# A two-stream transformer and state-space step on one core: the x chunks of groups 1 to 7 multiplied with high and low tokens side by side

## The chip, the cores and the metric

The kernel runs on one core of one Trainium2 chip. The metric is the device time of one execution in microseconds (us). The engines named here are TensorE (PE; its weight loads are PEld), VectorE (DVE), ScalarE (ACT), GpSimd (POOL) and SyncE (SP), which issues most of the loads of weights.

## The reference

Two streams of 128 tokens each (context and latent) go through two layers of width 2048. What matters here is the state-space branch of a layer:

```python
q, k, v, z_a, xbc, z_s, dt_f, dt_b, g_a, g_s = split_cols(h @ w_in, IN_SPLITS)
xbc = jax.nn.silu(centred_conv(xbc, conv_w, conv_b))      # 5 taps over the tokens, per channel
xs, b_ssm, c_ssm = split_cols(xbc, (SSD_WIDTH, BC_WIDTH, BC_WIDTH))
...
y = y_f + jnp.flip(y_b, 1) + d_skip[:, None].astype(x4.dtype) * x4
y = y.reshape(bsz, length, SSD_WIDTH) * jax.nn.silu(z_s)
yg = rmsnorm(y.reshape(bsz, length, N_SSD_GROUPS, SSD_WIDTH // N_SSD_GROUPS), ...)
```

`xs` has 4096 channels in 8 groups of 512. For each group the kernel computes its 512 columns of `h @ w_in` (a chunk called x), the convolution over the tokens, and then the two scans, which are matrix products with decay matrices.

## The kernel before, in words

**Chunks and halves.** Every product with a weight matrix is cut into chunks of 512 output columns, and a chunk into 8 halves (pieces of 256 x 512 weights, 128 x 1024 numbers in a tile). SyncE loads a half into one of 5 slots of `raw`. ScalarE rounds it into `w_h` (fp32r; `hi_half`, L473), VectorE forms the rest `w_l = raw - w_h` (`lo_half`, L478), and TensorE multiplies (`mm_half`): weights high times tokens high, weights high times tokens low, weights low times tokens high. `w_h` and `w_l` are rings of 4: ScalarE may split half k when TensorE has finished half k - 4 (semaphore `w_used`). Each engine's program is written out by hand: after half i of a chunk it does the steps listed for i. I number the 16 halves of a group 0 to 15.

**A group.** In the state-space stage a group g has two chunks: x (halves 0 to 7, channels on the partitions, accumulated in `pair(0)`, the first two banks of `PM`) and z_s (halves 8 to 15, tokens on the partitions, in the last two banks of `PM`). Between those halves the engines also do the scan of group g - 1. The steps that matter:

- TensorE: `y_start` and `xt_T` after half 0, `y_T` after 3, `y_diag` of two heads after 5, 7, 9 and 11 (into banks 0 and 1 of `A`; L816), `final_states` after 14 (into banks 2 and 3 of `A`).
- ScalarE: `z_silu` and `stores` after half 2, `clamp` (L1340) and `exp` (L1348) of four pairs of heads after 2 to 10, where the exponentials of the third and fourth pair wait for `y_diag` after halves 5 and 7, `y_hi` after 7 (L1355), the centre tap of the convolution after 11 (`conv`, L1394), its SiLU after 15 (L1401), then `squares` (L1369), which waits for VectorE's `add_y`. The split of half 0 of the next group stands behind `squares`.
- VectorE: `M` of the four pairs after 5, 7, 9 and 11 (three TENSOR_TENSOR each, L1601), `y_lo` after 8 (L1882), the four other taps after 12 and 13 (`conv_1`, `conv_2`, 16 instructions, L1645), `add_y` after 15 (three TENSOR_TENSOR).

**Another form that the kernel already has.** For the four z_a chunks of the attention stage `mm_wide` (L531 and L538) is used. A wide half holds 4 pieces of 128 rows by 256 columns: it multiplies each weight tile with high and low tokens side by side in one instruction of 512 columns (the two sums lie in the two halves of a bank), and only w_l times high tokens in one of 256. A chunk then has 4 halves for its first 256 channels and 4 for its last.

Of the kernel before, what the change touches and what calls it, by code (L numbers as in the profile page):

```python
# [17 lines left out]
ALU = mybir.AluOpType  # L18
# [5 lines left out]
TOK = 128  # L24
# [7 lines left out]
NG = 8  # L32
# [19 lines left out]
PH_SSD = PH_BC + 4  # L52
# [8 lines left out]
U_SSD = U_BC + 2  # L61
# [126 lines left out]
Z_RUN, Z_LOAD = z_tiles()  # L188


WIDE_BLOCKS = [B_ZA + g for g in range(4)]


def raw_order():
# [91 lines left out]
def build(nc, a, o):  # L286
    with ExitStack() as ctx:
# [505 lines left out]
        def _(pe):  # L793
# [33 lines left out]
            def layer(L, more):  # L827
# [175 lines left out]
                def ssd_steps(q):  # L1003
# [6 lines left out]
                    st[7] = st[7] + [lambda: banks_back(q)]  # L1010
                    return st

                def ssd_body(g, steps):
                    halves(base + PH_SSD + g * 2, "ch", 0, ub + U_SSD + g, hT_h, hT_l, steps)
# [155 lines left out]
        def _(act):  # L1170
# [40 lines left out]
            def layer(L, more):  # L1211
# [175 lines left out]
                def conv(g):  # L1387
                    chunk_done(act, base + PH_SSD + g * 2)
                    act.wait_ge(s_("chw_ready"), L + 1)
                    act.wait_ge(s_("conv_silu"), L * 12 + 4 + g)  # L1390
                    if g:
                        act.wait_ge(s_("xt_T"), L * NG + g)
                    for t in range(4):
                        mm = act.activation(xc[:, t * 256:(t + 1) * 256].rearrange("p (s n) -> p s n", s=2),  # L1394
                                            psum_sub(pair(0), t), F.Identity,
                                            bias=taps(5, 4 * g + t), scale=taps(2, 4 * g + t))
                    mm.then_inc(s_("conv_center"), 1)

                def silu(g):
# [186 lines left out]
        def _(dve):  # L1586
# [96 lines left out]
            def layer(L, more):  # L1683
# [70 lines left out]
                def conv_bc(k, half):  # L1754

                    freed, done, uses = ((bank_free[1], ub + U_BC + 2, 1), (bank_free[0], ub + U_BC + 3, 2),
                                         (s_("c_banks_read"), L + 1, 1), (bank_free[1], ub + U_BC + 3, 1))[k]
                    if half == 0:
                        dve.wait_ge(s_("conv_center"), L * 12 + k + 1)
# [127 lines left out]
                def ssd_steps(q):  # L1887
# [5 lines left out]
                        st[5 + 2 * p] = [lambda p=p: M(q, p)]  # L1893
                    return st

                def conv_1(g):
                    dve.wait_ge(s_("conv_center"), L * 12 + 4 + g + 1)
                    conv_taps(pair(0), 4 * g, bank_free[0], (0, 1))

                def conv_2(g):  # L1900
                    conv_taps(pair(0), 4 * g, bank_free[0], (3, 4))
                    dve.wait_ge(bank_free[0], ub + U_SSD + g + 2)
                    dve.sem_inc(s_("conv_done"), 1)

                def ssd_body(g, steps):
                    st = {k: list(v) for k, v in steps.items()}
                    st[12] = [lambda: conv_1(g)] + st.get(12, [])
                    st[13] = [lambda: conv_2(g)] + st.get(13, [])
# [377 lines left out]
```

## Time and profile before

| | |
|---|---|
| median of 3 runs | 2758.02 us (2757.69 to 2758.1) |
| the profiled execution | 2757.51 us, its span 2755.6 us |
| granted clock of TensorE, mean over the span | 0.996 |
| busy: PE, PEld, DVE, ACT, POOL | 98%, 83%, 72%, 54%, 6% |

The span is the time from the first to the last instruction; the profiled execution's own time is 1.9 us longer. Busy time is the sum of the instructions' spans; matmuls overlap in it. A timeline row gives the start and length of a run of like instructions, and in brackets how long the engine had been idle and what ended that.

### The profile page before, as it was taken

Reading aid. Unit: us, or ns where it says so; the run is one execution under the profiler, and the core shown is the slowest. Engines: PE = TensorE matmul, PEld = TensorE weight load, DVE = VectorE, ACT = ScalarE, POOL = GpSimd, SP = SyncE. Lnnn points to the kernel's source line nnn. Section 1 sums busy time; section 2 is a strip of 40 time slices with the busy share of each in tenths; the row PEclk is TensorE's granted clock in tenths of the full one; section 3 lists DMA queues with packets and bytes.
Section 4 is the critical chain, followed back from the end, with each engine's and each line's share of the span. In section 5 each row is a group of like instructions: output and inputs, shape, how many; then the busy total and the mean of one; then the engine's idle time right before and its main releaser. Section 6 shows DMA issues by size and latency. Waiting matters only on the chain.

```text
span 2755.6 us, 38506 instructions
## 1 busy us (share of the span) xinstructions
PE 2704.9 (98%) x15312; PEld 2297.9 (83%) x15312; DVE 1975.6 (72%) x2308; ACT 1490.4 (54%) x2161; POOL 172.5 (6%) x242
## 2 busy tenths in 40 slices
PE   6999999999999999999999999999999999999998
PEld 4898898888887888888879898889888888888886
DVE  2488788887997667688865788888866644655555
ACT  3366877785333455534434677787644344555443
POOL 0000101111000000000110011110110000000000
PEclk9999999999999999999999999999999999999999
DMA  9956666666987655587885666576566664545665
GB/s 393 345 178 219 218 223 211 201 226 233 316 307 274 229 192 191 187 289 264 306 282 174 202 221 222 191 234 219 190 229 237 244 199 161 176 160 184 201 218 168
DMA packets 175668, 627.84 MB, mean 228 GB/s; under 512 B 21029, under 2 KB 23333, under 8 KB 175105
## 3 DMA queue, kind: packets, MB, share of 16 engines
q1 hardware_dynamic: 154944, 557.19, 58.3%
q0 software_dynamic: 10672, 33.30, 4.2%
q10 hardware_dynamic: 9872, 34.89, 4.0%
q8 instruction: 121, 1.98, 0.3%
q14 instruction: 59, 0.48, 0.1%
HBM read 611.37 MB, written 13.93 MB: 227 GB/s over the span
## 4 chain that ended last, share of the span: by engine, by line
PE 88%; DVE 6%; DMA 3%; ACT 2%; issue 1%; SPq 0%; DVEq 0%; POOLq 0%; POOL 0%; ACTq 0%
PE PM L500 19%; PE PM L512 19%; PE PM L501 19%; PE A L816 6%; PE PM L516 5%; PE PM L505 5%; PE PM L506 5%; PE A L531 2%; PE PM L531 2%; DMA Zt<-in_w_mod 2%; DVE w_l L478 1%; DVE arena L598 1%; DVE X L1645 1%; DMA raw<-in_w_in 1%; PE PM L538 1%
## 5 line engine op out<-in xcount | busy, mean ns | idle before, releaser
L478 DVE TENSOR_TENSOR w_l<-raw,w_h 128x1024 fp32r<-128x1024 f32 (+1 forms) x880 | 1059.2, 1222 | 653.2 <-ACT w_h L473 645.7
L473 ACT ACTIVATE w_h<-raw 128x1024 fp32r<-128x1024 f32 (+1 forms) x880 | 905.5, 1046 | 759.0 <-PE PM L512 565.1
L500 PE MATMUL PM<-w_h,hT 128*128 128x512 f32 x1408 | 563.5, 400 | 2.1 <-issue 1.8
L501 PE MATMUL PM<-w_h,hT 128*128 128x512 f32 x1408 | 549.2, 390 | 0.0
L500 PE MATMUL PM<-w_h,Z 128*128 128x512 f32 x1016 | 399.2, 393 | 0.8 <-issue 0.8
L501 PE MATMUL PM<-w_h,Z 128*128 128x512 f32 x1016 | 395.6, 389 | 0.0
L512 PE MATMUL PM<-w_l,hT 128*128 128x512 f32 x1408 | 377.3, 390 | 0.0
L505 PE MATMUL PM<-hT,w_h 128*128 128x256 f32 x1408 | 350.6, 287 | 3.3 <-DVE X L1645 1.7
L506 PE MATMUL PM<-hT,w_h 128*128 128x256 f32 x1408 | 344.8, 283 | 0.0
L500 PEld LDWEIGHTS PM<-w_h,hT 128*128 128x128 f32 x1408 | 264.6, 188 | 59.7 <-issue 7.8
L512 PEld LDWEIGHTS PM<-w_l,hT 128*128 128x128 f32 x1408 | 264.2, 188 | 57.0 <-DVE w_l L478 0.4
L501 PEld LDWEIGHTS PM<-w_h,hT 128*128 128x128 f32 x1408 | 264.6, 188 | 55.8 <-issue 3.3
L505 PEld LDWEIGHTS PM<-hT,w_h 128*128 128x128 f32 x1408 | 269.2, 191 | 9.8 <-issue 5.5
L512 PE MATMUL PM<-w_l,Z 128*128 128x512 f32 x1016 | 272.5, 390 | 2.4 <-DVE w_l L478 2.4
L506 PEld LDWEIGHTS PM<-hT,w_h 128*128 128x128 f32 x1408 | 269.6, 192 | 0.5
L500 PEld LDWEIGHTS PM<-w_h,Z 128*128 128x128 f32 x1016 | 190.7, 188 | 44.2 <-issue 5.1
L512 PEld LDWEIGHTS PM<-w_l,Z 128*128 128x128 f32 x1016 | 190.1, 188 | 44.3 <-DVE w_l L478 4.5
L501 PEld LDWEIGHTS PM<-w_h,Z 128*128 128x128 f32 x1016 | 190.8, 188 | 40.1 <-issue 1.0
L516 PE MATMUL PM<-hT,w_l 128*128 128x256 f32 x1408 | 197.8, 283 | 0.9 <-DVE w_l L478 0.9
L516 PEld LDWEIGHTS PM<-hT,w_l 128*128 128x128 f32 x1408 | 181.6, 192 | 1.3 <-DVE w_l L478 1.3
L1340 ACT ACTIVATE Zt<-Zt,SA 128x128 f32<-128x128 f32 x512 | 162.5, 391 | 1.0 <-DMA Zt<-acs_scratch 0.9
L1601 DVE TENSOR_TENSOR arena<-arena 128x512 f32<-128x512 f32 (+2 forms) x158 | 142.4, 901 | 5.4
(215 smaller groups left out, 2612.1 us busy)
## 6 DMA issues: line engine op xcount, KB each, us to landing
raw<-in_w_in SPq DMA_DIRECT2D x608, 512.0 KB, 4.5
raw<-in_w_ps SPq DMA_DIRECT2D x128, 512.0 KB, 4.6
Zt<-in_w_mod SPq DMA_DIRECT2D x104, 512.0 KB, 13.2
arena<-in_w_mod SPq DMA_DIRECT2D x72, 512.0 KB, 6.5
Zt<-acs_scratch ACTq DMA_DIRECT2D x64, 512.0 KB, 4.8
raw<-in_w_pa SPq DMA_DIRECT2D x64, 512.0 KB, 4.2
raw<-in_w_out SPq DMA_DIRECT2D x64, 512.0 KB, 5.5
arena<-in_states POOLq DMA_DIRECT2D x16, 512.0 KB, 7.5
```

Source lines behind the costliest of these rows:

```text
L473: act.activation(w_h[:, k % RING, :, 0:n], half_raw(k, n), ACT.Copy).then_inc(hi_ready, 1)
L478: dve.tensor_tensor(w_l[:, k % RING, :, 0:n], half_raw(k, n), w_h[:, k % RING, :, 0:n].bitcast(F32), ALU.subtract).then_inc(lo_ready, 1)
L500: pe.matmul(tok_out(s), hi[:, kt, tk], wh, start=kt == 0, stop=False, skip_group_check=True)
L501: pe.matmul(tok_out(s), lo[:, kt, tk], wh, start=False, stop=False, skip_group_check=True)
L505: pe.matmul(ch_out(t), wh[:, cs], hi[:, kt], start=kt == 0 and t % 2 == 0, stop=False, skip_group_check=True)
L506: pe.matmul(ch_out(t), wh[:, cs], lo[:, kt], start=False, stop=False, skip_group_check=True)
L512: mm = pe.matmul(tok_out(s), hi[:, kt, s * TOK:(s + 1) * TOK], wl, start=False, stop=kt == last_kt, skip_group_check=True)
L516: mm = pe.matmul(ch_out(t), wl[:, t * P:(t + 1) * P], hi[:, kt], start=False, stop=kt == last_kt, skip_group_check=True)
L531: pe.matmul(banks[:, t, :].rearrange("p (x n) -> p x n", x=2), w[0][:, at:at + P], hT[:, :, kt], start=kt == 0, stop=False, skip_group_che ...
L816: return pe.matmul(out, lhsT, rhs, start=start, stop=stop, skip_group_check=True)
L1340: ins = act.activation(rows_of[:, ds], rows_of[:, ds], F.Relu, scale=-1.0, bias=SA[:, ds, q * HG + h:q * HG + h + 1])
L1601: return dve.tensor_tensor(out, a_, b_, op)
```

## The change

The x chunks of groups 1 to 7, in both layers, are done by `mm_wide`. Halves 0 to 3 of the chunk go into `pair(0)` and halves 4 to 7 into banks 2 and 3 of `A`. Weights of these blocks are laid out for it ahead of the launch. The high and low sums then have to be added: ScalarE copies the low sum of two tiles to `x_low` in `Zt` (`copy_low`, after half 8 and after half 11), VectorE adds it to the high sum in PSUM, in place (`sum_x`, after half 10 and after half 11), ScalarE makes the centre tap in two parts (`center_x`, after halves 11 and 12), and VectorE the other taps, from PSUM, in two parts (`conv_x`, after halves 12 and 13). Group 0 stays as it was.

```diff
-WIDE_BLOCKS = [B_ZA + g for g in range(4)]
+WIDE_BLOCKS = [B_XBC + g for g in range(1, NG)] + [B_ZA + g for g in range(4)]
...
+        def x_summed_at(t):
+            return (PM if t < 2 else A)[:, t, 0:256].rearrange("p (s n) -> p s n", s=2)
...
                 def final_states(q):
                     if q:
                         pe.wait_ge(s_("st_stored"), L * NG + q)
+                    if q < NG - 1:
+                        pe.wait_ge(s_("conv_done"), L * 12 + 4 + q + 2)
...
+                def x_wide(g, steps):
+                    c = base + PH_SSD + g * 2
+                    bank_wait(pe, 0, ub + U_SSD + g)
+                    for i in range(8):
+                        if i == 4 and g > 1:
+                            pe.wait_ge(s_("st_stored"), L * NG + g - 1)
+                        mm_wide(pe, c, i, pair(0) if i < 4 else A[:, 2:4, :])
...
+                def copy_low(g, part):
+                    chunk_done(act, base + PH_SSD + g * 2, 4 + 4 * part)
+                    if part == 0:
+                        act.wait_ge(s_("conv_done"), L * 12 + 4 + g)
+                    banks = A[:, 2:4, :] if part else pair(0)
+                    act.activation(x_low[:, part * 512:(part + 1) * 512]..., banks[:, :, 256:512], F.Copy)
+                def center_x(g, part):
+                    if part == 0:
+                        act.wait_ge(s_("conv_silu"), L * 12 + 4 + g)
+                        act.wait_ge(s_("xt_T"), L * NG + g)
+                    act.wait_ge(s_("x_summed"), 2 * (L * (NG - 1) + g - 1) + part + 1)
+                    for t in (2 * part, 2 * part + 1):
+                        mm = act.activation(x_tile(xc, t), x_summed_at(t), F.Identity, bias=..., scale=...)
...
-                    st[11] = [lambda: conv(g)] + st.get(11, [])
+                    if g:
+                        st[8] = st.get(8, []) + [lambda: copy_low(g, 0)]
+                        st[11] = [lambda: copy_low(g, 1), lambda: center_x(g, 0)] + st.get(11, [])
+                        st[12] = [lambda: center_x(g, 1)] + st.get(12, [])
...
+                def sum_x(g, part):
+                    dve.wait_ge(s_("x_low_copied"), 2 * (L * (NG - 1) + g - 1) + part + 1)
+                    high = A[:, 2:4, 0:256] if part else PM[:, 0:2, 0:256]
+                    tt(high, high, low, ALU.add).then_inc(s_("x_summed"), 1)
+                def conv_x(g, part):
+                    tiles = (2 * part, 2 * part + 1)
+                    ...
+                            ins = dve.scalar_tensor_tensor(out=o_, in0=x_summed_at(t)[:, :, lo_ + d:hi_ + d], ...)
+                    ins.then_inc(s_("conv_done") if part else bank_free[0], 1)
...
+                    if g:
+                        st[10] = st.get(10, []) + [lambda: sum_x(g, 0)]
+                        st[11] = [lambda: sum_x(g, 1)] + st.get(11, [])
+                        st[12] = [lambda: conv_x(g, 0)] + st.get(12, [])
+                        st[13] = [lambda: conv_x(g, 1)] + st.get(13, [])
```

On ScalarE, from the exponential of the third pair (L1348 before, L1373 now) to the split of half 12, these rows stood in group 2 before (L473 is the split into `w_h`, L1340 a clamp, L1394 the centre tap):

```order
L1348 ACTIVATE arena<-Zt 128x1024 [waits act_chain,y_part]
L1340 ACTIVATE Zt<-Zt,SA 128x128 [waits decays_loaded1]
L1340 ACTIVATE Zt<-Zt,SA 128x128 x3
L473 ACTIVATE w_h<-raw 128x1024 [waits w_used,raw_loaded2]
L1277 DMA Zt<-acs_scratch 128x1024 [waits exp_done]
L1340 ACTIVATE Zt<-Zt,SA 128x128 x4
L473 ACTIVATE w_h<-raw 128x1024 [waits w_used,raw_loaded3]
L1348 ACTIVATE arena<-Zt 128x1024 [waits act_chain,y_part]
L473 ACTIVATE w_h<-raw 128x1024 [waits w_used,raw_loaded4]
L1394 ACTIVATE X<-PM,chw 128x256 [waits conv_silu,xt_T,chw_ready,w_used]
L1394 ACTIVATE X<-PM,chw 128x256 x3
```

And now (L475 is the split, L1365 a clamp, L1428 the copy of a low sum, L1437 the centre tap):

```order
L1373 ACTIVATE arena<-Zt 128x1024 [waits act_chain,y_part]
L1365 ACTIVATE Zt<-Zt,SA 128x128 [waits decays_loaded1]
L1365 ACTIVATE Zt<-Zt,SA 128x128 x3
L1428 ACTIVATE Zt<-PM 128x512 [waits conv_done,w_used]
L475 ACTIVATE w_h<-raw 128x1024 [waits w_used,raw_loaded2]
L1302 DMA Zt<-acs_scratch 128x1024 [waits exp_done]
L1365 ACTIVATE Zt<-Zt,SA 128x128 x4
L475 ACTIVATE w_h<-raw 128x1024 [waits w_used,raw_loaded3]
L1373 ACTIVATE arena<-Zt 128x1024 [waits act_chain,y_part]
L475 ACTIVATE w_h<-raw 128x1024 [waits w_used,raw_loaded4]
L1428 ACTIVATE Zt<-A 128x512 [waits w_used]
L1437 ACTIVATE X<-PM,chw 128x256 [waits x_summed,xt_T,conv_silu]
```

The first copy of a low sum stands ahead of the split of half 9, the second behind that of half 11, and the centre tap now waits for VectorE.

On VectorE, from the split of half 10 to the split of half 14, these rows stood in group 2 before (L478 the split into `w_l`, L1645 the taps):

```order
L478 TENSOR_TENSOR w_l<-raw,w_h 128x1024 [waits hi_ready] x2
L1601 TENSOR_TENSOR arena<-arena,SA 128x1024 [waits exp_done]
L1601 TENSOR_TENSOR arena<-arena 128x1024 [waits dve_chain]
L1601 TENSOR_TENSOR arena<-arena 128x2x256 [waits dve_chain]
L478 TENSOR_TENSOR w_l<-raw,w_h 128x1024 [waits hi_ready]
L1645 SCALAR_TENSOR_TENSOR X<-PM,chw,X 128x2x126 [waits conv_center]
L1645 SCALAR_TENSOR_TENSOR X<-PM,chw,X 128x2x126 x3
L1645 SCALAR_TENSOR_TENSOR X<-PM,chw,X 128x2x127 [waits dve_chain] x4
L478 TENSOR_TENSOR w_l<-raw,w_h 128x1024 [waits hi_ready]
L1645 SCALAR_TENSOR_TENSOR X<-PM,chw,X 128x2x127 [waits dve_chain] x4
L1645 SCALAR_TENSOR_TENSOR X<-PM,chw,X 128x2x126 [waits dve_chain] x4
L478 TENSOR_TENSOR w_l<-raw,w_h 128x1024 [waits bank_free0,hi_ready]
```

And now (L480 the split, L1647 the sums and products, L1961 the taps):

```order
L480 TENSOR_TENSOR w_l<-raw,w_h 128x1024 [waits hi_ready]
L1647 TENSOR_TENSOR PM<-PM,Zt 128x2x256 [waits x_low_copied]
L480 TENSOR_TENSOR w_l<-raw,w_h 128x1024 [waits hi_ready]
L1647 TENSOR_TENSOR A<-A,Zt 128x2x256 [waits x_low_copied]
L1647 TENSOR_TENSOR arena<-arena,SA 128x1024 [waits exp_done]
L1647 TENSOR_TENSOR arena<-arena 128x1024 [waits dve_chain]
L1647 TENSOR_TENSOR arena<-arena 128x2x256 [waits dve_chain]
L480 TENSOR_TENSOR w_l<-raw,w_h 128x1024 [waits hi_ready]
L1961 SCALAR_TENSOR_TENSOR X<-PM,chw,X 128x2x126 [waits x_summed,conv_center]
```

Two sums stand ahead of the fourth `M`, and the split of half 14 no longer waits for `bank_free0`, which the second part of the taps used to release and wait for.

## Rows read from the trace of the kernel before

**Rows 1.** The page, busy time, share of the span and instructions of each engine.
```profile
PE 2704.9 (98%) x15312; PEld 2297.9 (83%) x15312; DVE 1975.6 (72%) x2308; ACT 1490.4 (54%) x2161; POOL 172.5 (6%) x242
```

**Rows 2.** What TensorE waited for: us in total, times, longest.
```profile
PE PM L505 <- ACT w_h L473: 1.0, 2, 0.5
```

**Rows 3.** Busy time by engine in one group: PE, PEld, DVE, ACT, POOL, PEclk, DMA.
```profile
332.76:386.47 53.71, 53.71 (x346) 47.80 (x344) 45.87 (x59) 40.48 (x72) 6.84 (x8) 1.00 0.64 216
```

**Rows 4.** Timeline of TensorE: start us, length us, line, count.
```profile
332.76 0.28 PE L505 MATMUL PM<-hT,w_h 128*128 128x256 f32 x1
...
349.63 1.12 PE L516 MATMUL PM<-hT,w_l 128*128 128x256 f32 x8
352.51 1.12 PE L516 MATMUL PM<-hT,w_l 128*128 128x256 f32 x8
353.48 1.00 PE L816 MATMUL A<-X,arena 128*128 128x64 f32 x8
...
360.12 1.00 PE L816 MATMUL A<-X,arena 128*128 128x64 f32 x8
...
386.47 0.28 PE L505 MATMUL PM<-hT,w_h 128*128 128x256 f32 x1
...
547.59 0.28 PE L505 MATMUL PM<-hT,w_h 128*128 128x256 f32 x1
...
601.72 0.47 PE L500 MATMUL PM<-w_h,hT 128*128 128x512 f32 x1 [0.26 <-issue]
```

**Rows 5.** Timeline of ScalarE in the same group, and one row at 599 us.
```profile
328.76 0.63 ACT L1369 ACTIVATE arena<-X 128x512 f32<-128x512 f32 x1 [4.50 <-DVE X L1601]
...
352.67 1.07 ACT L473 ACTIVATE w_h<-raw 128x1024 fp32r<-128x1024 f32 x1
354.51 1.06 ACT L1348 ACTIVATE arena<-Zt 128x1024 f32<-128x1024 f32 x1 [0.78 <-PE A L816]
...
356.65 1.05 ACT L473 ACTIVATE w_h<-raw 128x1024 fp32r<-128x1024 f32 x1
...
361.16 1.06 ACT L1348 ACTIVATE arena<-Zt 128x1024 f32<-128x1024 f32 x1 [1.34 <-PE A L816]
...
382.46 0.63 ACT L1369 ACTIVATE arena<-X 128x512 f32<-128x512 f32 x1 [4.50 <-DVE X L1601]
...
384.11 2.96 ACT L473 ACTIVATE w_h<-raw 128x1024 fp32r<-128x1024 f32 x3
...
599.17 2.96 ACT L473 ACTIVATE w_h<-raw 128x1024 fp32r<-128x1024 f32 x3 [0.17 <-issue]
```

**Rows 6.** Timeline of VectorE in the same group.
```profile
355.69 1.65 DVE L1882 SCALAR_TENSOR_TENSOR Z<-PM,chw,Z 128x256 fp32r<-128x256 f32 x4
357.73 1.23 DVE L478 TENSOR_TENSOR w_l<-raw,w_h 128x1024 fp32r<-128x1024 f32 x1 [0.39 <-ACT w_h L473]
...
361.99 2.44 DVE L478 TENSOR_TENSOR w_l<-raw,w_h 128x1024 fp32r<-128x1024 f32 x2
...
373.61 3.19 DVE L1645 SCALAR_TENSOR_TENSOR X<-PM,chw,X 128x254 f32<-128x254 f32 x8
376.94 2.36 DVE L478 TENSOR_TENSOR w_l<-raw,w_h 128x1024 fp32r<-128x1024 f32 x2
...
381.20 1.23 DVE L1601 TENSOR_TENSOR X<-X 128x1024 f32<-128x1024 f32 x1
```

**Rows 7.** Waits of ScalarE for VectorE, whole span: us in total, times, longest.
```profile
ACT arena L1369 <- DVE X L1601: 69.9, 16, 4.5
```

**Rows 8.** Timeline of TensorE in a z_a chunk.
```profile
949.99 2.00 PE L531 MATMUL PM<-hT,w_h 128*128 128x512 f32 x8
...
952.78 2.00 PE L531 MATMUL PM<-hT,w_h 128*128 128x512 f32 x8
```

**Rows 9.** A pair of half-size VectorE products (timeline), and ScalarE's copies in z_a (source view).
```profile
342.98 1.28 DVE L1601 TENSOR_TENSOR arena<-A,SA 128x512 f32<-128x512 f32 x2
...
L1514 ACT ACTIVATE arena<-PM x8: 598/598/599, 958.6 to 2458.4; 128x512 f32<-128x512 f32 x8
```

More of the change, by code:

```diff
@@ L323, in part @@
             return arena[:, at:at + n]
+        CENTERS = 5 + 2 * (NG - 1)
         BCX = part(4352, 0).rearrange("p (t n) -> p t n", n=256)
@@ L334, in build @@
         decay_rows = [Zt[:, 7, :], Zt[:, 15, :]]
+        x_low = Zt[:, 6, :]
         def CB(q):
@@ L693, in psum_sub, with x_tile @@
             return banks[:, t // 2, (t % 2) * 256:(t % 2 + 1) * 256].rearrange("p (s n) -> p s n", s=2)
+        def x_tile(held, t):
+            return held[:, t * 256:(t + 1) * 256].rearrange("p (s n) -> p s n", s=2)
+        def x_summed_at(t):
+            return (PM if t < 2 else A)[:, t, 0:256].rearrange("p (s n) -> p s n", s=2)
         def x_banks(q):
@@ L1011, in ssd_steps @@
                     return st
+                def x_wide(g, steps):
[5 more added lines that the diff above has]
+                        mm_wide(pe, c, i, pair(0) if i < 4 else A[:, 2:4, :])
+                        tiles_behind(K(c, i))
+                        for step in steps.get(i, ()):
+                            step()
                 def ssd_body(g, steps):
-                    halves(base + PH_SSD + g * 2, "ch", 0, ub + U_SSD + g, hT_h, hT_l, steps)
+                    if g:
+                        x_wide(g, steps)
+                    else:
+                        halves(base + PH_SSD, "ch", 0, ub + U_SSD, hT_h, hT_l, steps)
                     halves(base + PH_SSD + g * 2 + 1, "tok", 1, ub + U_SSD + g, hT_h, hT_l, steps, first=8)
@@ L1390, in conv @@
                     act.wait_ge(s_("conv_silu"), L * 12 + 4 + g)
-                    if g:
-                        act.wait_ge(s_("xt_T"), L * NG + g)
                     for t in range(4):
@@ L1396, in conv @@
                                             bias=taps(5, 4 * g + t), scale=taps(2, 4 * g + t))
+                    mm.then_inc(s_("conv_center"), 1)
+                def copy_low(g, part):
[3 more added lines that the diff above has]
+                    banks = A[:, 2:4, :] if part else pair(0)
+                    act.activation(x_low[:, part * 512:(part + 1) * 512].rearrange("p (t n) -> p t n", t=2), banks[:, :, 256:512], F.Copy)                        .then_inc(s_("x_low_copied"), 1)
+                def center_x(g, part):
[4 more added lines that the diff above has]
+                    for t in (2 * part, 2 * part + 1):
+                        mm = act.activation(x_tile(xc, t), x_summed_at(t), F.Identity, bias=taps(5, 4 * g + t), scale=taps(2, 4 * g + t))
                     mm.then_inc(s_("conv_center"), 1)
@@ L1758, in conv_bc @@
                     if half == 0:
-                        dve.wait_ge(s_("conv_center"), L * 12 + k + 1)
+                        dve.wait_ge(s_("conv_center"), L * CENTERS + k + 1)
                     conv_taps(bc_banks(k), 32 + 4 * k, freed, ((0, 1), (3, 4))[half], uses)
@@ L1894, in ssd_steps @@
                     return st
+                def sum_x(g, part):
+                    dve.wait_ge(s_("x_low_copied"), 2 * (L * (NG - 1) + g - 1) + part + 1)
+                    low = x_low[:, part * 512:(part + 1) * 512].rearrange("p (t n) -> p t n", t=2)
+                    high = A[:, 2:4, 0:256] if part else PM[:, 0:2, 0:256]
+                    tt(high, high, low, ALU.add).then_inc(s_("x_summed"), 1)
+                def conv_x(g, part):
+                    tiles = (2 * part, 2 * part + 1)
+                    dve.wait_ge(s_("conv_center"), L * CENTERS + 5 + 2 * (g - 1) + part + 1)
+                    dve.wait_ge(s_("x_summed"), 2 * (L * (NG - 1) + g - 1) + part + 1)
+                    for j in (0, 1, 3, 4):
+                        d = j - 2
+                        lo_, hi_ = max(0, -d), TOK - max(0, d)
+                        for t in tiles:
+                            if j > 0:
+                                ch.wait(tap_done[t])
+                            o_ = x_tile(xc, t)[:, :, lo_:hi_]
+                            ins = dve.scalar_tensor_tensor(out=o_, in0=x_summed_at(t)[:, :, lo_ + d:hi_ + d], scalar=taps(j, 4 * g + t),
+                                                           in1=o_, op0=ALU.mult, op1=ALU.add)
+                            if not (j == 4 and t % 2):
+                                tap_done[t] = ch.link(ins)
+                    ins.then_inc(s_("conv_done") if part else bank_free[0], 1)
                 def conv_1(g):
-                    dve.wait_ge(s_("conv_center"), L * 12 + 4 + g + 1)
+                    dve.wait_ge(s_("conv_center"), L * CENTERS + 5)
                     conv_taps(pair(0), 4 * g, bank_free[0], (0, 1))
@@ L1906, in ssd_body @@
                     st = {k: list(v) for k, v in steps.items()}
-                    st[12] = [lambda: conv_1(g)] + st.get(12, [])
-                    st[13] = [lambda: conv_2(g)] + st.get(13, [])
+                    if g:
+                        st[10] = st.get(10, []) + [lambda: sum_x(g, 0)]
+                        st[11] = [lambda: sum_x(g, 1)] + st.get(11, [])
+                        st[12] = [lambda: conv_x(g, 0)] + st.get(12, [])
+                        st[13] = [lambda: conv_x(g, 1)] + st.get(13, [])
+                    else:
+                        st[12] = [lambda: conv_1(g)] + st.get(12, [])
+                        st[13] = [lambda: conv_2(g)] + st.get(13, [])
                     halves(base + PH_SSD + g * 2, st)
```

2 lines of the change are left out of this document (added).

## The prediction

> **What bounds the kernel now.** I read the page first: TensorE is busy for 98% of the span, VectorE for 72%, ScalarE for 54% [rows 1]. The waits of TensorE are next: in the whole program it waited for ScalarE's split 1.0 us in 2 waits ahead of the matmuls of an x chunk [rows 2]. So TensorE sets the time, and one group of the state-space stage, from the first matmul of its half 0 at 332.76 to that of the next at 386.47, takes 53.71 us [rows 3, 4], with no gap.
>
> That it never waits doesn't say how near it is to waiting. For that I followed the two engines that feed it. After the scan of a group ScalarE sits idle for 4.50 us until VectorE has ended `add_y`, then does `squares`, and only behind that splits half 0 of the next group [rows 5]. All 16 `squares` wait like this, 69.9 us in total [rows 7], so the pattern repeats at every boundary. The first of the three splits starts at 384.11 and, at some 1.06 us each, has ended at 385.17; TensorE needs it at 386.47. The slack is 1.30 us.
>
> From one `squares` to the next there is thus a loop through ScalarE and VectorE, and I measure it. I call the start of `squares` S (328.76).
> - ScalarE works without a gap from S to the split of half 8, which ends at 353.74 [rows 5]. The next ACTIVATE could start 0.10 earlier than that (three splits of 1.05 take 2.96), at S + 24.88. It started at 354.51, for it waited 0.78 us for `y_diag`, which ended at 353.48 + 1.00 [rows 4].
> - From there to the split of half 9 are 2.14 us (356.65 - 354.51), and its end is 1.05 later.
> - VectorE is ready for half 9 when `y_lo` has ended (355.69 + 1.65, less its overlap of 0.08), at S + 28.50; it waited 0.39 us for that split and started at 357.73 [rows 6].
> - From 357.73 VectorE is busy to the end of `add_y` (381.20 + 1.23), and `squares` starts at 382.46: 24.73 us.
>
> If TensorE never held it, the loop would take 28.50 + 24.73 = 53.23 us, just 0.48 less than TensorE's 53.71. The kernel has two limits here that lie within 1% of each other.
>
> **The change, part by part.**
> 1. TensorE's saving. A half of the x chunk takes 352.51 - 349.63 = 2.88 us, 24 matmuls of 256 columns [rows 4]. A wide half, 8 of 512 and 8 of 256, takes 952.78 - 949.99 = 2.79 [rows 8]. That is 0.09 a half, 0.72 a group, 10.1 us over 14 chunks. TensorE's own time for a group falls to 52.99.
> 2. ScalarE's first copy of a low sum. Such a copy takes 598 ns [rows 9], 0.50 less the overlap. It stands ahead of the split of half 9. That split then ends at S + 24.88 + 2.14 + 0.50 + 1.05 = S + 28.57 and VectorE starts on it at S + 28.60, against S + 28.50: plus 0.10 on the loop (where `y_diag` was the last to come, as in group 1, plus the whole 0.50).
> 3. VectorE's two sums. No row shows a sum written to PSUM. The nearest are two 512-element products with one operand from PSUM in 1.28 us, 0.60 each with the overlap [rows 9]. I take 0.60 each, so plus 1.20: both stand in VectorE's unbroken stretch. Bounds: a single-input pass of this size costs about 0.4, and a sum at half rate would be like one of twice the elements, 1.23 with 0.08 overlap, 1.15. That makes 0.8 to 2.3 for the two. Nothing at all is excluded, since the stretch has no gap to hide them in.
> 4. What goes. The splits of halves 10 and 11 now take 2.44, of which 0.08 is a wait for ScalarE (2 x 1.22 less overlap is 2.36); behind the first sum that wait is gone: minus 0.08. Between the last tap (373.61 + 3.19 = 376.80) and the split of half 14 (376.94) lie 0.14, where the overlap would be 0.08; the wait for `bank_free0` there is gone: minus 0.22.
> 5. At no cost: the second copy (after half 11; VectorE needs it three microseconds later), the centre tap in two parts (four instructions before and after, its wait for the sums falls into ScalarE's idle time, and the taps need it only behind `M`), the 16 taps (two tiles at a time, so an instruction depends on the one two before it, 0.78 us earlier, and one takes under 0.5). TensorE's new wait for `st_stored` at half 4 is covered, because ScalarE stores ahead of the split of half 3, and that for `conv_done` because the split of half 14 stands behind the same taps. Loads keep their sizes and order. If the cover of the centre tap were gone, its two instructions, 0.9, would come onto the loop.
>
> **The sum.** The loop becomes 28.60 + 24.73 + 1.20 - 0.08 - 0.22 = 54.23 us, above TensorE's 52.99 and above 53.71. Is `y_diag` then still early enough? TensorE starts half 0 at S + 2.71 (385.17 - 382.46). `y_diag` ended 354.48 - 332.76 = 21.72 after that start, now 0.54 less (six shorter halves): S + 23.89, before ScalarE's S + 24.88. The fourth pair: 361.12 - 332.76 - 0.72 + 2.71 = S + 30.35, ScalarE comes at S + 24.88 + 5.31 + 0.50 = S + 30.69 (5.31 is 361.16 - 1.34 - 354.51). So the loop holds itself, and TensorE waits for the split of half 0, 54.23 - 52.99 = 1.24 us a group.
>
> By boundary, in each layer:
> - Out of group 1, whose ScalarE has no stores and waits for `y_diag`: the split comes 0.50 + 1.20 - 0.30 = 1.40 later, TensorE is 0.18 earlier (two halves after `y_diag`), the slack was 1.30: a wait of 0.28. Net -0.72 + 0.28 = -0.44.
> - Groups 2 to 6: 54.23 - 53.71 = +0.52 each, +2.60.
> - Group 7, into the next stage: it took 601.72 - 547.59 = 54.13, and ScalarE pays 0.2 more at the end of the phase (0.17 of idle time ahead of its splits) [rows 4, 5]: 54.23 + 0.2 - 54.13 = +0.3.
>
> That is +2.5 a layer, +5.0 in all. The later stages have no such loop and keep what they are given. The profiled execution's 2757.5 would become 2762.5; the runs' median lies 0.5 above it, so I forecast **2763.0 us**. 0.2% of this kernel, about what a measurement can tell from no change, is 5.5 us: the forecast lies just inside it, on the slow side.
>
> A rule would make TensorE's part smaller. The row gives 0.09 us a half. The Trainium skill, VectorE: DVE Perf Modes, in its section on the TRN2 errata, has a matmul take 6 cycles plus its columns; by it 8 x 216 + 8 x 109 ns against 24 x 109 would save 0.02 us a half, 2 us in all, and the sum would end at about 2764, since the saving counts in group 1 alone. The trace has its own durations, and I use those.
>
> **The rivals.**
> - *TensorE's saving comes through.* For it speaks that TensorE is busy for all 53.71 us of a group and VectorE for 45.87 (85%), which the sums raise to 47.1 [rows 3]: by busy shares there is room. It holds if the loop stays below 52.99. It is 53.23 - 0.30 = 52.93 without the new work, so the new work would have to cost under 0.1 where I count 1.30. Then the time is 2758.0 - 10.1 = 2747.9. Against it speak the loop's gapless rows. The Trainium skill, Perfetto Trace Analysis, section Identifying the Most-Contended Engine, says to find the limit by occupancy and work on that engine first; by that rule it is TensorE, and this rival is what it gives. Chance 12% for over 0.2% faster.
> - *Loop and saving cancel.* The added work comes to about 0.8 us a loop in place of 1.30: 53.73 a group, as before, and about 2757. It decides at this price of 0.8: below it the kernel gains, above it it loses. Chance 20%.
> - *The loop as worked out*, 2763, its own range 2759 to 2768. Chance 50%.
> - *Slower by more: sums in PSUM at half rate.* At 1.15 each the loop grows by 1.10 more, 54.23 + 1.10 = 55.33, in six boundaries of a layer, with the first too: 14 x 1.1 = 15 us, 2778. Also here belongs the split of half 14, at S + 50.0 against TensorE's need at S + 50.3, by my sum: if that is missed, TensorE waits in mid-group, which its 1.24 of waiting at half 0 pays for until it's used up. Chance 18% for above 2768.
>
> **How the numbers follow.** The likeliest case gives 2763.0. Between 2756 and 2770 lie the loop, most of the cancelling case and the lower third of the last one, some 8 in 10. Faster by over 0.2% (below 2752.5): 0.12. Slower by over 0.2% (above 2763.5): the upper part of the loop's case, 0.25, and the last, 0.18, makes 0.43. Within: 0.45.
>
> **What the changed profile would show.** Right: groups 2 to 6 some 54.2 us apart; TensorE idle for 1.2 us at each boundary until ScalarE's split, about 12 waits; the wide halves 2.79 apart; VectorE's sums 0.68 long; ScalarE's exponential of the third pair no longer waiting for `y_diag`. Wrong: groups at 53.0 with no idle TensorE (the saving came through), sums of over 1 us, a gap ahead of the sums or taps (a copy or centre tap is late), or waits in mid-group at halves 4 or 14. The forecast is wrong above all if the price of the sums or the overlaps of 0.1 are off: each 0.1 us in the loop is 1.4 us in the total.

## The result, and the profile after

The changed kernel takes **2762.16 us** (median of 14 runs, 2761.02 to 2765.98), the kernel before 2758.19 (14 runs, 2757.16 to 2759.03) beside it. The ratio is 1.0016, with a 95% interval of 1.0009 to 1.0024: slower by 4.0 us, or 0.16%. Forecast were 2763.0 and a range of 2756 to 2770. The profiled execution took 2761.81 us, its span 2760.0.

The page of after, busy time by engine, answers to [rows 1]; under it stands the line of section 4, the chain that ended last by engine:

```profile
PE 2702.2 (98%) x14416; PEld 2253.2 (82%) x14416; DVE 1990.6 (72%) x2336; ACT 1501.3 (54%) x2189; POOL 172.1 (6%) x242
...
PE 67%; DVE 21%; ACT 5%; issue 4%; DMA 3%; SPq 0%; DVEq 0%; ACTq 0%; POOLq 0%; POOL 0%
```

TensorE does 896 matmuls fewer and is busy for 2.7 us less, in a program that takes 4 us more. The shares look like those of before. The chain does not: VectorE now holds 21% of it, and in the chain of before it held 6%:

```profile
PE 88%; DVE 6%; DMA 3%; ACT 2%; issue 1%; SPq 0%; DVEq 0%; POOLq 0%; POOL 0%; ACTq 0%
```

This share is a hint and no price: experiment 1 has one nearly as large without a wait at half 0. What TensorE waited for at half 0 (us in total, times, longest) answers to [rows 2]:

```profile
PE PM L533 <- ACT w_h L475: 8.9, 12, 1.1
```

That is the predicted number of waits: six boundaries in each of the two layers. (The seventh, out of group 7, leads to a chunk of another form and stands at L502.) The windows view of group 2, half 0 to half 0 (length, then PE, PEld, DVE, ACT, POOL, granted clock, DMA share, GB/s), answers to [rows 3]:

```profile
332.52:386.65 54.13, 53.31 (x280) 44.40 (x281) 46.84 (x61) 41.28 (x74) 6.83 (x9) 1.00 0.66 214
```

A group takes 54.13 us where it took 53.71, at a granted clock of 1.00, the level of 2.4 GHz, and TensorE has gaps in it. Its timeline shows them at the first matmul of half 0 (L533). The columns are start, length, line and count, and in brackets the idle time and what ended it; this answers to [rows 4]. (The last row is cut off at the end of the view, so it counts 3 of its 8 matmuls.)

```profile
332.52 2.09 PE L533 MATMUL PM<-hT,w_h 128*128 128x512 f32 x8 [0.85 <-ACT w_h L475]
...
337.91 2.09 PE L533 MATMUL PM<-hT,w_h 128*128 128x512 f32 x8
...
340.79 2.00 PE L533 MATMUL PM<-hT,w_h 128*128 128x512 f32 x8
...
343.58 2.00 PE L533 MATMUL PM<-hT,w_h 128*128 128x512 f32 x8
...
352.84 1.00 PE L824 MATMUL A<-X,arena 128*128 128x64 f32 x8
...
386.65 0.94 PE L533 MATMUL PM<-hT,w_h 128*128 128x512 f32 x3 [0.82 <-ACT w_h L475]
```

The wide form does work faster: half 2 follows at 340.79 and half 3 at 343.58, 2.79 apart, against 2.88 before. But half 0 now waits for ScalarE's split, at every boundary. ScalarE's timeline of the same group answers to [rows 5]:

```profile
329.66 0.63 ACT L1394 ACTIVATE arena<-X 128x512 f32<-128x512 f32 x1 [4.32 <-DVE X L1647]
...
354.51 1.06 ACT L1373 ACTIVATE arena<-Zt 128x1024 f32<-128x1024 f32 x1
356.63 0.59 ACT L1428 ACTIVATE Zt<-PM 128x512 f32<-128x512 f32 x1
357.11 1.06 ACT L475 ACTIVATE w_h<-raw 128x1024 fp32r<-128x1024 f32 x1
...
364.41 0.56 ACT L1437 ACTIVATE X<-PM,chw 128x256 f32<-128x256 f32 x1 [1.56 <-DVE PM L1647]
...
383.79 0.63 ACT L1394 ACTIVATE arena<-X 128x512 f32<-128x512 f32 x1 [4.32 <-DVE X L1647]
...
385.45 2.96 ACT L475 ACTIVATE w_h<-raw 128x1024 fp32r<-128x1024 f32 x3
```

The first of the three splits takes some 1.06 us and ends at 386.51; TensorE starts at 386.65. The slack at half 0, 1.30 before, is 0.14 at all seven boundaries of a layer: so much remains when the split is what is waited for. The exponential of the third pair (354.51) no longer has a bracket: `y_diag`, ended at 352.84 + 1.00 = 353.84, is not awaited any more. From one `squares` to the next are 383.79 - 329.66 = 54.13 us, exactly TensorE's period. VectorE's timeline answers to [rows 6]:

```profile
356.59 1.66 DVE L1928 SCALAR_TENSOR_TENSOR Z<-PM,chw,Z 128x256 fp32r<-128x256 f32 x4
358.20 1.23 DVE L480 TENSOR_TENSOR w_l<-raw,w_h 128x1024 fp32r<-128x1024 f32 x1
...
363.60 0.69 DVE L1647 TENSOR_TENSOR PM<-PM,Zt 128x512 f32<-128x512 f32 x1
364.20 1.22 DVE L480 TENSOR_TENSOR w_l<-raw,w_h 128x1024 fp32r<-128x1024 f32 x1
365.34 0.69 DVE L1647 TENSOR_TENSOR A<-A,Zt 128x512 f32<-128x512 f32 x1
365.94 1.22 DVE L1647 TENSOR_TENSOR arena<-arena,SA 128x1024 f32<-128x1024 f32 x1
...
375.19 3.19 DVE L1961 SCALAR_TENSOR_TENSOR X<-A,chw,X 128x252 f32<-128x252 f32 x8
378.30 2.35 DVE L480 TENSOR_TENSOR w_l<-raw,w_h 128x1024 fp32r<-128x1024 f32 x2
...
382.54 1.22 DVE L1647 TENSOR_TENSOR X<-X 128x1024 f32<-128x1024 f32 x1
```

There is no bracket in the whole stretch from 356.59 to 382.54: VectorE doesn't wait once. Each sum takes 0.69, and the next instruction starts 0.60 after the start of the sum.

### The profile page after: what moved, and what is told of

It is laid out like the page before. It is cut to its first block, busy times and chain, and to the rows that moved or that the text cites. A ratio compares the mean times of both kernels' runs of the same rounds, so it can differ in the third digit from the quotient of the medians.

```text
span 2760.0 us, 36798 instructions
## 1 busy us (share of the span) xinstructions
PE 2702.2 (98%) x14416; PEld 2253.2 (82%) x14416; DVE 1990.6 (72%) x2336; ACT 1501.3 (54%) x2189; POOL 172.1 (6%) x242
## 4 chain that ended last, share of the span: by engine, by line
PE 67%; DVE 21%; ACT 5%; issue 4%; DMA 3%; SPq 0%; DVEq 0%; ACTq 0%; POOLq 0%; POOL 0%
PE PM L502 15%; PE PM L514 15%; PE PM L503 15%; DVE w_l L480 6%; DVE arena L1647 4%; PE PM L533 4%; PE A L824 4%; PE A L533 4%; DVE arena L600 3%; PE PM L540 2%; PE A L540 2%; ACT w_h L475 2%; DVE X L1961 2%; DMA Zt<-in_w_mod 2%; DVE X L600 1%
## 5 line engine op out<-in xcount | busy, mean ns | idle before, releaser
L480 DVE TENSOR_TENSOR w_l<-raw,w_h 128x1024 fp32r<-128x1024 f32 (+1 forms) x880 | 1060.1, 1223 | 640.3 <-ACT w_h L475 635.2
L475 ACT ACTIVATE w_h<-raw 128x1024 fp32r<-128x1024 f32 (+1 forms) x880 | 905.2, 1046 | 730.8 <-PE PM L514 540.3
L502 PE MATMUL PM<-w_h,hT 128*128 128x512 f32 x1408 | 563.9, 400 | 3.6 <-ACT w_h L475 2.1
L502 PE MATMUL PM<-w_h,Z 128*128 128x512 f32 x1016 | 399.5, 393 | 0.8 <-issue 0.8
L502 PEld LDWEIGHTS PM<-w_h,hT 128*128 128x128 f32 x1408 | 264.8, 188 | 61.1 <-issue 9.3
L502 PEld LDWEIGHTS PM<-w_h,Z 128*128 128x128 f32 x1016 | 190.8, 188 | 44.1 <-issue 5.1
L533 PE MATMUL PM<-hT,w_h 128*128 128x512 f32 x704 | 180.7, 399 | 8.9 <-ACT w_h L475 8.9
L533 PE MATMUL A<-hT,w_h 128*128 128x512 f32 x704 | 179.2, 397 | 0.0
L1365 ACT ACTIVATE Zt<-Zt,SA 128x128 f32<-128x128 f32 x512 | 162.5, 392 | 0.2 <-DMA Zt<-acs_scratch 0.2
L533 PEld LDWEIGHTS PM<-hT,w_h 128*128 128x128 f32 x704 | 127.1, 189 | 39.2 <-issue 16.5
L1647 DVE TENSOR_TENSOR arena<-arena 128x512 f32<-128x512 f32 (+2 forms) x158 | 142.4, 901 | 5.3
L533 PEld LDWEIGHTS A<-hT,w_h 128*128 128x128 f32 x704 | 126.4, 189 | 22.5
L507 PE MATMUL PM<-hT,w_h 128*128 128x256 f32 x512 | 128.1, 288 | 3.3 <-DVE X L1691 1.7
L508 PE MATMUL PM<-hT,w_h 128*128 128x256 f32 x512 | 125.4, 283 | 0.0
```

The costliest lines, as they stand in the source:

```text
L475: act.activation(w_h[:, k % RING, :, 0:n], half_raw(k, n), ACT.Copy).then_inc(hi_ready, 1)
L480: dve.tensor_tensor(w_l[:, k % RING, :, 0:n], half_raw(k, n), w_h[:, k % RING, :, 0:n].bitcast(F32), ALU.subtract).then_inc(lo_ready, 1)
L502: pe.matmul(tok_out(s), hi[:, kt, tk], wh, start=kt == 0, stop=False, skip_group_check=True)
L507: pe.matmul(ch_out(t), wh[:, cs], hi[:, kt], start=kt == 0 and t % 2 == 0, stop=False, skip_group_check=True)
L508: pe.matmul(ch_out(t), wh[:, cs], lo[:, kt], start=False, stop=False, skip_group_check=True)
L533: pe.matmul(banks[:, t, :].rearrange("p (x n) -> p x n", x=2), w[0][:, at:at + P], hT[:, :, kt], start=kt == 0, stop=False, skip_group_che ...
```

## The experiments

The theory on trial: the loop from `squares` through the scan's splits, VectorE's unbroken stretch and back to `squares` sets the time of a group, because the split of half 0 stands behind `squares` on ScalarE. The rivals: the wide form or the sums' traffic in PSUM hold TensorE by themselves; the place of `squares` costs something in any case; VectorE or ScalarE have simply too much to do. The kernel before took 2757.95 us beside the first four kernels (15 runs, 2756.77 to 2759.41) and 2757.98 beside the last four (15 runs, 2756.74 to 2758.7).

**1. The two sums left out.** This kernel leaves the low sum of x out of the result; copies, the centre tap, the taps and all semaphores stay.

```diff
-                    tt(high, high, low, ALU.add).then_inc(s_("x_summed"), 1)
+                    dve.sem_inc(s_("x_summed"), 1)
```

> The changed kernel without VectorE's 28 sums of the low to the high product of x: the copied low sum is left out of the computation, all waits and copies stay. Loop theory (the loop from one squares to the next through ScalarE and VectorE, 54.13 us measured in the changed kernel, sets the group): it shrinks by two sums of 0.60 to about 52.95, under TensorE's own time for a group, which is 53.1 to 53.15 by the idle 0.99 us of each boundary. Groups 2 to 6 come 53.1 to 53.2 apart, TensorE hardly waits at half 0, and the time is about 2750 us. Rival (the wide form itself costs the time, by its waits for PSUM banks and the later release of them): the sums are hidden, and the time stays within 2 us of 2762.

Measured: 2749.36 us (2748.11 to 2749.84), ratio to before 0.9968 (0.9955 to 0.9980). TensorE's timeline at two boundaries:

```profile
330.92 1.98 PE L533 MATMUL PM<-hT,w_h 128*128 128x512 f32 x8
...
383.96 1.98 PE L533 MATMUL PM<-hT,w_h 128*128 128x512 f32 x8
```

The groups are 53.04 apart here (53.03 on the mean of the layer), the bracket is gone, and the 8 matmuls take 1.98 instead of 2.09. The slack at half 0 is 0.98. So the wide form costs nothing hidden, and TensorE's own time for a group is 53.03: the saving is 0.68 a group. Two instructions of 0.69 us on an engine that is busy for 72% of the span hold back the whole of it. This alone doesn't separate the loop from "too much work on VectorE"; the next kernel does. The page's chain of this kernel, where TensorE waits at no half 0, still gives much to the two feeding engines, so their share of the chain isn't the time that they cost:

```profile
PE 63%; DVE 17%; ACT 12%; issue 5%; DMA 2%; SPq 0%; ACTq 0%; DVEq 0%; POOLq 0%; POOL 0%
```

**2. All the work kept, the loop cut.** `squares` moves behind the splits of halves 0 to 2 of the next group. It is what the split of half 0 stood behind; nothing is left out.

```diff
                     if q:
+                        st[2].insert(0, lambda: squares(q - 1))
                         st[2].append(lambda: stores(q - 1))
...
-                    if g:
-                        st[15].append(lambda: squares(g - 1))
```

> The changed kernel with ScalarE's squares of group g moved from behind half 15 to behind the split of half 2 of the next group. Nothing is left out. Loop theory: ScalarE makes three splits in the 4.3 us in which it waited for VectorE, so that 2.9 us leave the way from squares to the third exponential and the loop falls clearly under 53. TensorE is the limit again at 53.1 to 53.2 a group, its saving comes through, and the time is about 2750 us, faster than both kernels. Rival (the sums and copies lengthen VectorE's and ScalarE's work in a way that is paid wherever squares stand, or the wide form's own waits cost): 2760 to 2763.

Measured: 2748.53 us (2747.39 to 2749.81), ratio 0.9965 (0.9952 to 0.9977). TensorE's timeline, and ScalarE's at the end of the group:

```profile
331.62 1.98 PE L533 MATMUL PM<-hT,w_h 128*128 128x512 f32 x8
...
384.65 1.98 PE L533 MATMUL PM<-hT,w_h 128*128 128x512 f32 x8
```
```profile
378.07 2.01 ACT L475 ACTIVATE w_h<-raw 128x1024 fp32r<-128x1024 f32 x2 [0.25 <-remote]
380.43 1.06 ACT L475 ACTIVATE w_h<-raw 128x1024 fp32r<-128x1024 f32 x1 [0.34 <-PE PM L514]
382.14 0.63 ACT L1394 ACTIVATE arena<-X 128x512 f32<-128x512 f32 x1 [0.66 <-DVE X L1646]
```

The splits of halves 0 and 1 start at 378.07, the first of them ends at about 379.13, and half 0 is multiplied at 384.65: a slack of 5.5. ScalarE waits for VectorE only 0.66 where it waited 4.32, since it spends that time on splits. The windows view of a group says what "too much work" would have meant:

```profile
331.62:384.65 53.03, 53.03 (x281) 44.47 (x280) 46.87 (x61) 41.68 (x73) 7.88 (x9) 1.00 0.65 218
```

VectorE is busy for 46.87, with both sums, as in after (46.84), and the group takes 1.10 less. The amount of work didn't matter, its place in the loop did. This version beats both kernels: 9.4 us under the kernel before, where 14 chunks at 0.68 make 9.5.

**3. The same move on the kernel before**, with the same edit.

> The kernel before with squares moved in the same way. Nothing is left out. Loop theory: TensorE set its groups at 53.71 with 1.30 us of slack at half 0; more slack gives nothing, 2758.2 within 1 us. Rival (the place of squares costs something by itself, whatever the x chunk's form): 2 us or more faster, and then the gain of the second run would be no sign of the loop.

Measured: 2757.55 us (2756.98 to 2758.61), ratio 0.9999 (0.9990 to 1.0008). TensorE's timeline, and the split of half 0 on ScalarE's:

```profile
332.48 0.28 PE L505 MATMUL PM<-hT,w_h 128*128 128x256 f32 x1
...
386.19 0.28 PE L505 MATMUL PM<-hT,w_h 128*128 128x256 f32 x1
```
```profile
377.92 1.06 ACT L473 ACTIVATE w_h<-raw 128x1024 fp32r<-128x1024 f32 x1 [0.25 <-remote]
```

The groups stay 53.71 apart, with a slack of 7.2 at half 0. So the place of `squares` by itself is worth nothing; it pays only once TensorE needs less than the loop.

**4. The copies and sums on the kernel before.** The x chunk stays in its old form; ScalarE copies 512 columns of `A` after halves 8 and 11, and VectorE adds them in place after halves 10 and 11, where after has its copies and sums. They work on banks that nothing else uses at that time, and nothing of the output changes; in the first such group they take 384 columns.

```diff
+                        st[8] = st.get(8, []) + [lambda: copy_low(g, 0)]
+                        st[11] = [lambda: copy_low(g, 1), lambda: conv(g)] + st.get(11, [])
...
+                    if g:
+                        st[10] = st.get(10, []) + [lambda: sum_x(g, 0)]
+                        st[11] = [lambda: sum_x(g, 1)] + st.get(11, [])
```

> The kernel before with the new work alone: in groups 1 to 7 ScalarE copies two PSUM banks of 512 to the spare tile after halves 8 and 11 and VectorE adds them in PSUM after halves 10 and 11 (old final states, already stored, that nothing reads again), while the x chunk stays in its old form. Loop theory: the loop of 53.23 grows by 0.10 + 1.20 - 0.08 to 54.45 (54.35 if it is as much shorter than my sum as it was in the changed kernel), above TensorE's 53.71, so groups 2 to 6 come 54.3 to 54.5 apart and the time is about 2766. Rival (work on engines that are busy 85% and 75% of a group fits into their idle time): 2758.

Measured: 2766.54 us (2766.35 to 2768.74), ratio 1.0034 (1.0021 to 1.0046). TensorE's timeline at two boundaries:

```profile
334.75 0.36 PE L506 MATMUL PM<-hT,w_h 128*128 128x256 f32 x1 [0.43 <-ACT w_h L474]
...
389.11 0.36 PE L506 MATMUL PM<-hT,w_h 128*128 128x256 f32 x1 [0.43 <-ACT w_h L474]
```

They are 54.36 apart, TensorE waits for the same split, and the slack is the same 0.14. TensorE's own group is 0.68 longer here than in the changed kernel, but the time from group to group only by 0.23: the loop decides, not the matmuls. And the 0.23 has a place, in VectorE's timeline between the last tap and the split of half 14:

```profile
377.41 3.19 DVE L1658 SCALAR_TENSOR_TENSOR X<-PM,chw,X 128x254 f32<-128x254 f32 x8
380.74 2.36 DVE L479 TENSOR_TENSOR w_l<-raw,w_h 128x1024 fp32r<-128x1024 f32 x2
```

The taps end at 380.60 and the split starts 0.14 later, as before the change [rows 6]; in after it starts 0.08 ahead of their end. That is the wait for `bank_free0`, which this kernel keeps: 0.22, as the prediction had it.

**5. The sums doubled.** Each sum is made once more ahead of itself, into an unused slot of `Zt` in SBUF.

```diff
+                    tt(Zt[:, 14, part * 512:(part + 1) * 512]..., high, low, ALU.add)
                     tt(high, high, low, ALU.add).then_inc(s_("x_summed"), 1)
```

> The changed kernel with each of its 28 sums done twice, once more into a spare tile that nothing reads. Loop theory: a sum costs the loop its 0.60 to 0.61 us, so 1.21 more per group: groups 2 to 6 come 55.3 us apart in place of 54.13, TensorE waits 2.3 us at each boundary, and the time is 2762 + 14 x 1.21 = 2779. Rival (the extra time in the changed kernel is a fixed one per group, from the new waits between the engines, and the sums themselves are partly hidden): clearly less, 2762 to 2772.

Measured: 2779.56 us (2778.47 to 2780.07), ratio 1.0079 (1.0066 to 1.0092). VectorE's timeline, the two forms of the sum, and TensorE's timeline at two boundaries and at half 14:

```profile
366.09 0.68 DVE L1647 TENSOR_TENSOR Zt<-PM,Zt 128x512 f32<-128x512 f32 x1
366.69 0.69 DVE L1647 TENSOR_TENSOR PM<-PM,Zt 128x512 f32<-128x512 f32 x1
```
```profile
335.02 2.09 PE L533 MATMUL PM<-hT,w_h 128*128 128x512 f32 x8 [1.43 <-ACT w_h L475]
...
383.25 1.20 PE L514 MATMUL PM<-w_l,hT 128*128 128x512 f32 x4 [0.32 <-DVE w_l L480]
...
390.34 2.06 PE L533 MATMUL PM<-hT,w_h 128*128 128x512 f32 x8 [1.42 <-ACT w_h L475]
```

The groups are 55.32 apart (one, held up by a late transfer, took 56.37): 1.19 more than in after, for two more sums at 0.60. These sums are paid in full. The wait at half 0 grew by only about 0.6; the other part now stands in the middle of the group, where TensorE waits for VectorE's split of half 14 (0.32 in this row). The prediction had named that place as the next to give way. In after its split is there 0.76 ahead of TensorE (the sum had 0.3), here 0.06.

**6. The sums doubled and the loop cut**, the edits of 5 and 2 together.

> Doubled sums and squares behind the split of half 2, both. Loop theory: with squares out of the way the same 28 further sums, 17 us of VectorE's work, fit into VectorE's waits; the tightest place is the split of half 14, which had 1.40 us to spare with single sums and keeps 0.2. TensorE sets 53.03 a group, and the time is as with single sums, 2748 to 2750. Rival (VectorE's load as such has become the limit): 2755 or more.

Measured: 2748.65 us (2747.79 to 2750.17), ratio 0.9968 (0.9956 to 0.9981), as fast as experiment 2. TensorE's timeline:

```profile
331.81 1.98 PE L533 MATMUL PM<-hT,w_h 128*128 128x512 f32 x8
...
384.85 1.98 PE L533 MATMUL PM<-hT,w_h 128*128 128x512 f32 x8
```

The extra sums that cost 17 us in the loop cost nothing here. The slack is not unlimited: at half 14 VectorE's split is there just 0.21 ahead of TensorE.

**7. `squares` behind one split only**, to ask how far it has to move: `st[0].append(lambda: squares(q - 1))` in place of the line in `st[2]`.

> The changed kernel with squares moved behind the split of half 0 alone, not of half 2. Loop theory: only 0.95 us leave the way from squares to the third exponential, so the loop is 53.18 and still 0.15 over TensorE's 53.03, but TensorE no longer needs its split of half 0 from behind squares, and that of half 1 has 2.7 us more; the drift of 0.15 a group over six groups stays inside that. TensorE is the limit: 2748 to 2750. Rival (what counts is ScalarE's whole load in the 4.3 us gap, so one split of three gives a third of the gain): 2757 to 2759.

Measured: 2748.52 us (2747.64 to 2748.66), ratio 0.9966 (0.9953 to 0.9978). The groups are 53.03 apart. One split ahead of it is enough, but not for ever: the slack at half 0 shrinks from 5.49 to 4.88 over the groups of a layer, and that at half 14 from 1.40 to 0.69, some 0.1 a group. ScalarE's timeline shows why:

```profile
275.56 0.63 ACT L1394 ACTIVATE arena<-X 128x512 f32<-128x512 f32 x1 [2.98 <-DVE X L1646]
...
328.70 0.64 ACT L1394 ACTIVATE arena<-X 128x512 f32<-128x512 f32 x1 [2.98 <-DVE X L1646]
```

From one `squares` to the next are 53.14 us, 0.1 more than TensorE's 53.03; 53.18 was expected. The loop is still the longer one and eats the slack, but eight groups are too few for it to get through. With `squares` behind half 2 there is no such drift (5.50 at the first boundary and 5.50 at the sixth, half 14 at 1.40 in all groups but one, which has 1.14), so I would choose that place.

**8. The first copy behind the split of half 9**, for the 0.10 that it put on the loop.

```diff
-                        st[8] = st.get(8, []) + [lambda: copy_low(g, 0)]
+                        st[9] = [lambda: copy_low(g, 0)] + st.get(9, [])
```

> The changed kernel with ScalarE's first copy of the low sum behind the split of half 9 in place of ahead of it. Loop theory: in groups 2 to 6 the copy costs next to nothing where it is, for VectorE is ready for half 9 only at the time when the split ends, so the loop falls by 0.0 to 0.1 only (54.03 to 54.13); in group 1, where VectorE waits for it, the boundary to group 2 comes 0.3 to 0.5 earlier. In all 1 to 2 us, 2760 to 2761. Rival (the copy is paid in full, 0.50 a group): 2755.

Measured: 2760.35 us (2759.08 to 2762.08), ratio 1.0010 (1.0001 to 1.0019). ScalarE's timeline, and VectorE's:

```profile
356.35 1.06 ACT L475 ACTIVATE w_h<-raw 128x1024 fp32r<-128x1024 f32 x1
357.30 0.59 ACT L1428 ACTIVATE Zt<-PM 128x512 f32<-128x512 f32 x1
```
```profile
356.21 1.65 DVE L1928 SCALAR_TENSOR_TENSOR Z<-PM,chw,Z 128x256 fp32r<-128x256 f32 x4
357.78 1.21 DVE L480 TENSOR_TENSOR w_l<-raw,w_h 128x1024 fp32r<-128x1024 f32 x1
```

Now `y_lo` sets VectorE's start, not the split: the row behind it starts 0.08 ahead of its end. Most groups are 54.06 to 54.08 apart, some 0.06 less than in after. In each layer group 2 takes 53.95 or 53.97, some 0.17 less, and group 1 0.35 less (52.17 against 52.52 in layer 0). Ten groups (3 to 7) at 0.06, two at 0.17 and two at 0.35 make 1.6 us; the medians differ by 1.8. Two groups of the profiled execution took longer, 54.28 and 54.85; in both ScalarE waited for a late transfer (0.18 and 0.75). So the copy's place is a small term, as the sum had it, and the sums are nearly all of the loss.

## Why the prediction held, step by step

- **What bounds the kernel.** Two limits within 1% of each other: right. Experiment 3 shows that TensorE sets the time of before (nothing gained by cutting the loop), experiment 4 that the loop lies close behind it.
- **TensorE's saving**, forecast 0.72 a group, measured 0.68 (53.71 - 53.03, experiments 1 and 2): 9.5 us in place of 10.1. The two rows that I compared, 2.88 against 2.79, hold for a half that follows another. Behind other work the gain is less: half 1 stands behind `y_start` and `xt_T`. The trace of before has its first matmul and that of half 2 at

```profile
338.15 0.36 PE L505 MATMUL PM<-hT,w_h 128*128 128x256 f32 x1
...
341.10 0.28 PE L505 MATMUL PM<-hT,w_h 128*128 128x256 f32 x1
```

  that is 2.95, and now it takes 340.79 - 337.91 = 2.88: 0.07 in place of 0.09. Three halves of each x chunk (1, 4 and 6) stand so.
- **A rule on a matmul's length.** The Trainium skill, VectorE: DVE Perf Modes, section on the TRN2 errata, has a matmul take 6 cycles plus its columns; the estimate from it was 0.02 us saved a half. The runs don't agree: they show 0.68 / 8 = 0.085 a half, and the measurement decides.
- **The copy.** VectorE was to start on half 9 at S + 28.60 and started at 358.20 - 329.66 = S + 28.54. The exponential ahead of it, forecast at S + 24.88, came at S + 24.85. Experiment 8 puts the copy at 0.06 a loop (forecast 0.10) and 0.35 at the first boundary (forecast 0.50, the full copy).
- **The sums**, 0.60 each, were bounded between 0.8 and 2.3 for the two. Measured: 0.60 each, whether the result goes to PSUM or to SBUF (experiment 5), and 1.19 of loop for two of them.
- **What goes.** The rest of the loop was to take 24.73 + 1.20 - 0.08 - 0.22 = 25.63 and took 54.13 - 28.54 = 25.59.
- **The loop** therefore came to 54.13 where I had 54.23, against TensorE's 53.03 where I had 52.99. The wait is the difference of the two: 1.10 a boundary, forecast 1.24. The bracket shows 0.82 to 0.85 of it. Without a wait the first matmul starts 0.17 ahead of the end of the row before (384.65 against 383.74 + 1.08 in experiment 2), and behind a wait half 0 itself is 0.11 longer (from its start to that of half 1: 5.39 against 5.28).
- **At no cost.** The centre tap waits 1.56 for the sum, in ScalarE's idle time, and the taps behind it start without a bracket. `y_diag` came 0.67 ahead of ScalarE (forecast 0.99). TensorE's matmuls at half 4 (`A`, L533) and its `final_states` don't stand in the waits view at all.
- **By boundary**, layer 0: out of group 1, -0.33 (52.52 against 52.85; forecast -0.44). Groups 2 to 6, +0.42 each (forecast +0.52). Group 7, +0.22 (54.35 against 54.13; forecast +0.3). That is +2.0, and +2.2 in layer 1, where one group took 54.39: 4.2 of the 4.4 us by which the span grew, where I had 5.0. The ten middle boundaries at 0.10 less make 1.0 of the difference. The two out of group 1 give back 0.2: TensorE waits 0.36 there (52.52 against 52.16 in experiments 1 and 2), forecast 0.28. One cause is that the sum let TensorE start at the very end of a split, and it starts 0.14 later. So the total is nearer to the forecast than its terms are, by errors that partly cancel.
- **The rivals.** "The saving comes through" needed new work of under 0.1 in the loop, and got 1.2 from the sums alone; it comes true when the loop is cut (2748.5, forecast for the rival 2747.9). The rule of the Trainium skill, Perfetto Trace Analysis, section Identifying the Most-Contended Engine, names TensorE in both kernels by occupancy, and so it does by the busy share of the weight loads, by which that section judges TensorE's headroom (83% and 82%). In before the trace agrees; in after TensorE is still the busiest, 98%, and yet what it gained is lost to an engine that is busy for 72%. "Cancel" asked for 0.8 a loop; the sums exceed that. "Half rate" is out with 0.60 a sum.

The group of layer 1 that took 0.27 more than its neighbours has a cause in ScalarE's timeline: its clamp waits for a transfer of decays that lands late. The first row is from after, the second from experiment 2:

```profile
1756.19 1.28 ACT L1365 ACTIVATE Zt<-Zt,SA 128x128 f32<-128x128 f32 x4 [0.16 <-DMA Zt<-acs_scratch]
```
```profile
400.47 1.28 ACT L1365 ACTIVATE Zt<-Zt,SA 128x128 f32<-128x128 f32 x4 [0.84 <-DMA Zt<-acs_scratch]
```

Inside the loop such a wait is paid by the group: 0.16 of it cost 0.27 here, and 0.92 cost 1.05 in experiment 5. With the loop cut, 0.84 cost nothing: the slack at the next half 0 fell from 5.5 to 5.25, and the group took 53.03 as ever. The runs of the changed kernel are also spread over 5 us where those of before are spread over 2; late transfers that nothing absorbs would do that, but only the profiled execution can show them, so this is not shown.

What stays open is small: the 0.2 us between the sum over the groups and the growth of the span, and the rest of the difference out of group 1.

## What to carry to other kernels

Before an engine that never waits is made faster, measure its slack: follow each engine that feeds it from one period to the next, add up what that loop would take if the first engine never held it, and compare. Here 53.23 against 53.71 told that a saving of 0.7 could bring at most 0.5, and that new work of 1.2 on the feeding engine would cost more than it brings. Work that waits for a late result should not stand ahead of what the limiting engine needs next: with `squares` behind the splits the same change gains 9.4 us instead of losing 4.0. The loop also passes on every late transfer, which slack would absorb. And test such a move together with the change it makes room for, because on the kernel before it measures as nothing.

## What the runs showed of the hardware that was not expected

- A VectorE sum of 128x512 in fp32 with an operand from PSUM takes 0.68 us into SBUF and 0.69 into PSUM, and the next instruction starts 0.60 after its start either way. I had left up to 1.15 for it.
- A matmul run behind other work is longer than one behind its own kind: 8 wide matmuls take 2.06 to 2.09 behind a wait or behind other steps, 2.00 behind a half of their own kind, and 1.98 at half 0 where nothing is awaited. In the narrow form the first matmul behind such a break shows 0.36 against 0.28. The starts say the same: the half behind the break is followed 2.88 later, the others 2.79.
- A wait can wander. With the sums doubled 1.19 more had to be waited for in a group, and about 0.6 of it turned up at another half, behind another engine (VectorE's split of half 14 in place of ScalarE's of half 0).
